# Moving a 100 KB arena from 0 to 16 bytes behind a multiple of 128 in on-chip memory

## The reference, cut to what matters

```python
# first block: 16 meta tokens + 256 tokens = 272 tokens
h = h + token_mixer(rmsnorm(h))       # 4 retention heads + 4 mLSTM heads, both directions
h = h + expert_choice_ffn(rmsnorm(h)) # 16 experts, each takes its 34 best tokens, d_ff = 2816
h = rmsnorm(h)[:, 16:]

# second block: two layers
for layer in range(2):
    y = fox_shortconv_mixer(h) if layer == 0 else rglru_mixer(h)
    x = x + rmsnorm(y)
    x = x + rmsnorm(memory_cross_attention(rmsnorm(x), rmsnorm(mem)))
    g, u = split(rmsnorm(x) @ w_gu); x = x + rmsnorm((silu(g) * u) @ w_down)   # 2816 wide
```

## Time and profile before

| | us |
|---|---|
| median of 3 runs | 2214.91 |
| the three runs | 2213.81, 2214.91, 2219.47 |
| the profiled execution's own time | 2218.87 |
| its span, first to last instruction | 2217.1 |
| TensorE busy in the span | 2089.0 (94%) |
| VectorE, ScalarE busy | 778.8 (35%), 627.2 (28%) |
| mean granted clock of TensorE, share of full speed | 0.991 |
| moved from and to HBM | 725.27 MB, 327 GB/s over the span |

### The profile page before, as it was taken

One profiled execution on the slowest core, in us unless ns is written; L12 is line 12 of the kernel. 1 busy time (PEld: TensorE's weight loads), 2 busy tenths in 40 slices (PEclk: granted clock), 3 DMA queues, 4 the chain that ended last, 5 costly groups with the idle time before them and its releaser, 6 DMA issues.

```text
span 2217.1 us, 27202 instructions
## 1 busy us (share of the span) xinstructions
PE 2089.0 (94%) x12031; PEld 1301.6 (59%) x12031; DVE 778.8 (35%) x1144; ACT 627.2 (28%) x988; POOL 45.4 (2%) x74
## 2 busy tenths in 40 slices
PE   9999998898898999989899899889999999999999
PEld 9987443333333433434333233327989998988997
DVE  8984211011010111111011011016666555886663
ACT  6664100000000000000000000005555444865442
POOL 3201000000000000000000000000000000000000
PEclk9999999999999999999999999999999999999999
DMA  7548999999999999999999999997444655554653
GB/s 235 174 137 353 414 431 429 427 431 431 428 429 431 429 428 430 430 429 427 430 430 429 430 429 431 429 426 261 154 155 152 209 189 183 193 177 144 206 192 114
DMA packets 146527, 725.27 MB, mean 327 GB/s; under 512 B 8678, under 2 KB 106522, under 8 KB 119658
## 3 DMA queue, kind: packets, MB, share of 16 engines
q1 hardware_dynamic: 145224, 721.53, 81.3%
q0 software_dynamic: 640, 1.37, 0.2%
q10 hardware_dynamic: 546, 0.63, 0.1%
HBM read 722.44 MB, written 1.07 MB: 326 GB/s over the span
## 4 chain that ended last, share of the span: by engine, by line
PE 68%; DMA 27%; DVE 2%; ACT 1%; SPq 1%; issue 0%; DVEq 0%; ACTq 0%
PE bank L1396 24%; PE bank L1268 17%; DMA weight_ring<-in_w_up_dram 9%; DMA weight_ring<-in_w_gate_dram 9%; DMA weight_ring<-in_w_down_dram 8%; PE bank L1351 7%; PE bank L1235 5%; PE bank L885 4%; PE bank L1427 3%; PE bank L1199 1%; PE bank L1084 1%; PE bank L1326 1%; PE bank L1613 1%; PE bank L1743 1%; PE bank L1636 1%
## 5 line engine op out<-in xcount | busy, mean ns | idle before, releaser
L1268 PE MATMUL bank<-weight_ring,arena 128*64 128x506 f32 x3024 | 635.0, 565 | 61.0 <-DMA weight_ring<-in_w_up_dram 39.5
L1268 PEld LDWEIGHTS bank<-weight_ring,arena 128*64 128x64 f32 x3024 | 217.2, 135 | 462.9 <-issue 375.1
L1351 PE MATMUL bank<-weight_ring,arena 128*64 128x512 f32 x1408 | 319.8, 604 | 48.2 <-DMA weight_ring<-in_w_down_dram 48.2
L2917 DVE TENSOR_TENSOR weights_ring<-weight_ring,weights_ring 128x2048 fp32r<-128x2048 f32 x110 | 249.7, 2289 | 125.9 <-ACT weights_ring L2176 125.3
L1396 PE MATMUL bank<-input_high,weights_ring 128*128 128x256 f32 x1920 | 245.1, 280 | 0.8 <-issue 0.8
L1351 PEld LDWEIGHTS bank<-weight_ring,arena 128*64 128x64 f32 x1408 | 98.5, 138 | 249.5 <-issue 183.2
L1396 PEld LDWEIGHTS bank<-input_high,weights_ring 128*128 128x128 f32 x1920 | 231.5, 188 | 2.8 <-issue 2.6
L2176 ACT ACTIVATE weights_ring<-weight_ring 128x2048 fp32r<-128x2048 f32 x109 | 205.9, 1909 | 59.5 <-DMA weight_ring<-in_w_ffn_down_dram 40.7
L2874 DVE TENSOR_TENSOR arena<-arena,bank 128x512 f32<-128x512 f32 x48 | 33.0, 688 | 498.2 <-PE bank L1235 498.2
L2072 ACT ACTIVATE arena<-bank 128x506 f32<-128x506 f32 (+1 forms) x48 | 23.5, 562 | 398.7 <-PE bank L1268 398.7
L1396 PE MATMUL bank<-input_low,weights_ring 128*128 128x256 f32 x960 | 130.6, 279 | 0.0
(11 more groups left out here) (431 smaller groups left out, 2078.5 us busy)
## 6 DMA issues: line engine op xcount, KB each, us to landing
weight_ring<-in_w_down_dram SPq DMA_DIRECT2D x62, 2816.0 KB, 21.8
weight_ring<-in_w_up_dram SPq DMA_DIRECT2D x61, 2816.0 KB, 19.5
weight_ring<-in_w_gate_dram SPq DMA_DIRECT2D x60, 2816.0 KB, 18.9
weight_ring<-in_w_ffn_gu_dram SPq DMA_DIRECT2D x44, 1024.0 KB, 5.2
weight_ring<-in_w_ffn_down_dram SPq DMA_DIRECT2D x22, 1024.0 KB, 4.9
weight_ring<-in_w_in_dram SPq DMA_DIRECT2D x16, 1024.0 KB, 6.1
arena<-in_w_xkv_dram SPq DMA_DIRECT2D x8, 2048.0 KB, 21.1
weight_ring<-in_ab_w_in_dram SPq DMA_DIRECT2D x12, 1024.0 KB, 7.5
```

What stands on the lines that cost most here:

```text
L1268: last = pe.matmul(bank[first_bank + c][MPAD * half:MPAD * half + MPAD, 0:(hi - lo) * HF], xs3[:, s, :], w[:, lo:hi, HF * half:HF * half + ...
L1351: last = pe.matmul(bank[6][MPAD * half:MPAD * half + MPAD, :], hidT[:, at:at + MPAD], W[:, j * D + 512 * half:j * D + 512 * half + 512], s ...
L2917: dve.tensor_tensor(low_slot(k), raw_slot(k), high_slot(k), ALU.subtract).then_inc(S("weights_low"), 1)
```

## The change

The unused tile ahead of the arena grows from 24 to 28 columns, so that the arena begins at 128912, 16 bytes behind a multiple of 128, and each tile in it moves up by 16 bytes. Everything ahead of it stays. No instruction is added, removed, reordered or given another shape, and no wait changes; only start addresses do. 28 columns still fit: the arena ends at 229264.

```diff
@@ -156,7 +156,7 @@
         GW = sb("gate_w", KT * 16)
         RW = sb("router_w", KT * 16)
         small = sb("small", 184)
-        sb("arena_offset", 24)
+        sb("arena_offset", 28)
         Z = sb("arena", ARENA)
 
         def rounded(name, over, at, cols):
```

## The result

| | before | after |
|---|---|---|
| median, us | 2214.6 (4 runs, 2213.81 to 2219.47) | 2227.4 (4 runs, 2226.96 to 2227.47) |
| profiled execution, us | 2218.87 | 2227.41 |
| its span, us | 2217.1 | 2225.6 |

The ratio of the times is 1.0055, with a 95% interval of 1.0042 to 1.0067: slower by 12.8 us on the medians. The prediction was 2216 us in a range of 2209 to 2226, so the time lies outside it.

What follows compares the result with a forecast made beforehand. TensorE was taken to bound the first stage and last 700 us, HBM's stream the experts; all terms summed to 0 on 2218.87 us, and the forecast, set between that and the median 2214.91, was 2216 us, range 2209 to 2226.

Steps and rivals of the forecast that it cites:

- fp32r matmuls, moving operand in the arena: L1396's 2880 matmuls of 256 columns, TensorE-bound stage: taken at 0, bounds from -8.0 to -10.3 us up to +17.8 us.
- not a property of an address: L1396's paces of 117.9 and 113.5 ns on the same addresses were put down to how a stretch began.
- the quick pace is lost: Rival, layer 1's gate and up products: moving operand off a multiple of 128 costs +4.1 to +6.3 us, 2224 us; chance 0.24.
- no stretch over 850 in 100 us: Sign of the lost quick pace: no stretch passes 850 L1396 matmuls in 100 us, and the minimum is 279 ns or more.
- the 512-column matmuls with a stationary operand in the arena: L1396 with 512 columns: weight loads of 188 ns run beside the matmul before, so the cost was taken as 0.
- between the two: Forecast of 2216 us, placed between the profiled execution's 2218.87 us and the runs' median of 2214.91.
- DVE and ACT: Vector and activation work on arena tiles: 0 to 0.3 us would show, taken as 0.
- the fp32 matmuls: Experts' matmuls, median 586 ns at three offsets modulo 128: 0 to 1 us, taken as 0.
- the transfers: DMA loads into the arena and result stores: taken as 0; eight xkv loads at half speed would cost +39 us.
- The second rival (slow transfers): Transfers into the arena at half speed in the experts: +39 us, 2255 us; chance 0.07.
- over 188 ns: Sign: weight loads of L1396 or L1427 above 188 ns would show a start cost held for nothing.

Runs made afterwards that it cites:

- arena16: Kernel before with the arena's contents truly 16 bytes behind a multiple of 128, as slices 16 bytes further on; 2229.68 us, ratio 1.0045.
- after_x0: Changed kernel with input_high and input_low back at a multiple of 128, tiles behind them 128 bytes further on; 2225.11 us, ratio 1.0039.
- both32: Kernel before with ring and arena both 32 bytes further on, so their distance stays 64; 2220.79 us, ratio 1.0005.
- after_d64: Changed kernel with input_high and input_low 224 bytes further on, so the ring is again 64 bytes ahead modulo 256; 2215.56 us, ratio 0.9989.
- The maps: Runs without the kernel's computation: TensorE alone, series of 48 fp32r matmuls at varied moving/stationary starts modulo 256; spacing 113.3 to 123.4 ns with 256 columns.
- the map (L100): First map, TensorE alone, 28 pairs of starts with 256 moving columns; its line L100 has equal starts (0/0), 120.0 ns spacing.
- arena64: Kernel before with the unused tile at 40 columns, so the arena begins 64 bytes behind a multiple of 128 (distance 0); 2228.78 us, ratio 1.0056.

## Why the prediction was wrong

**The step that failed** is "fp32r matmuls, moving operand in the arena ... I take 0, the value if the paces are chosen as before". The paces were not chosen as before. In its place the runs showed that the spacing hangs on the starts of both operands: with the moving one at a multiple of 32 the distance modulo 256 sets it, and only some distances (52, 64 and 76, and 192 seldom) have the quick pace at all. At 64 a series takes the quick pace of 113.3 or the slow one of 117.8 as it begins, which is what the earlier trace rows showed; at 32 there is one of 118.4, and none quick. I had read the two paces on the same addresses as "not a property of an address". Whether there is a quick pace to be had is just that. That 32 bytes were built instead of 16 is not the reason: arena16, the true 16, took 2229.68 us and lies outside the range too.

**The rival that held** is "the quick pace is lost": its place (L1396, layer 1 above all) and its sign ("no stretch over 850 in 100 us": 844 and 847) were right, though the minimum rose only to 277 ns. Its mechanism was half right: it is not the moving operand's start off a multiple of 128 (after_x0, both32). It was given 2224 us and 0.24. Against the profiled execution's 2227.41 two terms were mis-sized: the spacing went to 118.4, not to 117.9 (2880 x 0.5 ns = 1.4 us), the 512-column matmuls with a stationary operand in the arena, taken at 0, cost 1.5 us more, and the rest is 0.5 us.

**Medians and levels.** I placed the forecast "between the two" times of before, and the rival on the profiled one. By the levels, the median of before stands for executions with both long stretches quick; the profiled one had one slow. after_d64 and both32 with both quick were at 2215.07 and 2216.82, before with one slow at 2218.87. The level near 2223 would be both slow; no profile of before fell there or at 2215, so both are inferences from the 4 us between levels. The rival should have been added to the slower level of both stretches, about 2223, and 118.4 ns and the 512-column term make 2226 of that, 1.5 us from the result.

**What held.** DVE and ACT at 0, the fp32 matmuls at 0, the transfers at 0: the earlier trace rows stayed, but for `w_up` into the arena, which landed 0.5 us sooner. The second rival (slow transfers) is excluded for a start 16 bytes off a multiple of 32 as well, by arena16's 21.6 us for `xkv` and 429 GB/s in the experts. The Trainium skill, "Collectives: The Full Stack", "Rules for kernel authors", asks for 32-byte alignment against a read-modify-write; arena16 breaks that alignment, and for these transfers of 16 KB in a piece it shows no such price.

**What could have been seen.** The Trainium skill, "TensorE: Matmul & The Clock Gate", "Step-by-step: what each phase is for", says that TensorE has two independent read ports and that loading the next tile's weights takes no read bandwidth from the running matmul. I had argued in the same sense from the 188 ns of the loads. The maps do not show who waits for whom, but the two are not without influence on each other: the spacing moves between 113.3 and 120.0 ns with where the two operands start against each other, and the loads do not keep 188 ns either. With 256 columns moving at distance 0 their median is 192, in the map (L100) as in arena64's L1396, the sign "over 188 ns" that I had named for a cost of the start. In the earlier trace rows, L1427 at 279 and L1396 at 276 or 281 were two distances, 192 and 64. I saw the difference, and looked at each start by itself and modulo 128; a map of pairs of starts could not be had blind, but a rival "both starts together" could, and would have had the same price as the lost pace and more chance. And I left out the rival that the change does not do what it says: the layout rounds 112 bytes to 128.

## What to carry to other kernels

When a kernel is bound by short fp32r matmuls, note where the moving and the stationary operand start modulo 256, keep the moving one at a multiple of 32 (the starts that these maps cover best), and treat a shift of either as a possible change of 2 to 6% in their rate. Shift whole groups of tiles together, or re-measure; 64 bytes between them served best with 256 columns, and equal starts with 512. If a kernel's runs fall into levels, find out which level the profiled one is in before a sum is hung on it.

## What the runs showed of the hardware that I had not expected

- The spacing of fp32r matmuls of 256 columns with a weight load of 128 each ranges from 113.3 ns to 123.4 by the starts of the operands, with TensorE alone and at a granted clock of 1.00; with 512 columns from 226.7 to 234.3.
- Some pairs of starts have two paces, and a series that has begun in one stays in it: 113.3 or 117.8 at distance 64, 113.3 or 120.0 at 76. For 192/116 and 192/244 the number of transposes ahead (even or odd) decided which, in all eight series. In the kernel a whole layer's 936 matmuls stay in one, which makes levels 4 us apart.
- The rule goes down to 4 bytes: 52 and 76 have the quick pace, 56, 60, 68, 72 and 80 not. I have no mechanism that gives these numbers; the table is all there is.
- The distance alone does not tell when the moving operand starts off a multiple of 32: at distance 76, 116/192 has 120.0 and once 123.4, never the quick pace, where 128/204 has 113.3 in six of eight series. 116/192 and its mirror 192/116 (113.8 or 118.1) differ as well, so it matters which of the two moves. Off a multiple of 32 is not always slow: 144/128 had 113.3 in two of four series.
- With 256 columns moving, the weight loads have a median of 192 ns at distance 0 and 188 or 189 at every other distance of the maps with the moving operand at a multiple of 16; at distance 112 and 160 the spacing is 120.0 all the same, so this is not the whole of it.
- Transfers of 2 MB into a start 16 bytes behind a multiple of 128 ran at full rate (21.6 us from issue to landing, against 21.1; 429 GB/s over 600 to 800 us, as before).
